# Two transformer blocks on one core: the first norm's root moved behind its projections, and the start reordered

## The reference

```python
def rmsnorm(x, g):
    xf = x.astype(jnp.float32)
    y = xf * lax.rsqrt(jnp.mean(xf * xf, axis=-1, keepdims=True) + EPS)
    return (y * g.astype(jnp.float32)).astype(x.dtype)

u = rmsnorm(h, norm_mix_g[layer])
p = jnp.einsum('bsd,de->bse', u, w_in[layer]) + b_in[layer]
aq, ak, av, hq, hf, hi, hg, gate_a, gate_b = split_columns(p)
y_attn = sliding_window_sink_attention(aq, ak, av, attn_sinks[layer])
y_hgrn = hgrn2_branch(hq, hf, hi, hg, lb_all[layer], hgrn_norm_g[layer])
```

## Time and profile before

| | us |
|---|---|
| median of 3 runs | 791.05 (790.83 to 791.09) |
| the profiled execution | 790.83 |
| its span | 789.1 |
| PE busy | 777.0 (98%) |
| DVE busy | 607.1 (77%) |
| ACT busy | 476.1 (60%) |

### The profile page before, as it was taken

The page is one execution under the profiler, slowest core; times in us unless marked ns, Lnnn a source line. Parts: engine busy times, 40 slices in busy tenths (PEclk is TensorE's granted clock), DMA queues, the critical chain, the costliest instruction groups (busy, mean ns, idle before and its releaser), DMA issues. The chain is left out here.

```text
span 789.1 us, 12516 instructions
## 1 busy us (share of the span) xinstructions
PE 777.0 (98%) x5048; PEld 687.0 (87%) x5048; DVE 607.1 (77%) x815; ACT 476.1 (60%) x727; POOL 18.6 (2%) x38
## 2 busy tenths in 40 slices
PE   8999999999999999999999999999999999999996
PEld 8978978898888898888888888999789999999885
DVE  5587788687887667887869897997878788777464
ACT  6855887568644384444334267876858667665451
POOL 3000002000200000000000000001000000000000
PEclk9999999999999999999999999999999999999999
DMA  8873644656546638799879993644363756555611
GB/s 302 296 261 127 227 138 149 208 186 215 174 161 213 214 107 283 269 305 315 276 242 339 336 380 126 222 135 133 108 213 111 237 175 200 167 172 170 240 53 54
DMA packets 106537, 162.54 MB, mean 206 GB/s; under 512 B 4576, under 2 KB 51824, under 8 KB 106480
## 3 DMA queue, kind: packets, MB, share of 16 engines
q1 hardware_dynamic: 106336, 161.48, 61.3%
q10 hardware_dynamic: 144, 0.26, 0.1%
HBM read 160.67 MB, written 1.06 MB: 205 GB/s over the span
## 5 line engine op out<-in xcount | busy, mean ns | idle before, releaser
L1175 DVE TENSOR_TENSOR wL<-raw,wH 128x2048 fp32r<-128x2048 f32 (+2 forms) x142 | 285.2, 2013 | 84.3 <-ACT wH L764 81.9
L764 ACT ACTIVATE wH<-raw 128x2048 fp32r<-128x2048 f32 (+1 forms) x114 | 212.1, 1864 | 91.7 <-PE ps L1866 61.1
L1863 PE MATMUL ps<-p1H,wH 128*128 128x256 f32 x784 | 224.0, 286 | 1.6 <-DVE arena L1175 0.8
L1863 PE MATMUL ps<-p1H,wL 128*128 128x256 f32 x784 | 221.2, 283 | 0.0
L1863 PE MATMUL ps<-p1L,wH 128*128 128x256 f32 x784 | 219.8, 283 | 0.0
L1863 PEld LDWEIGHTS ps<-p1H,wH 128*128 128x128 f32 x784 | 150.2, 192 | 5.5 <-DVE wL L1175 2.2
L1863 PEld LDWEIGHTS ps<-p1H,wL 128*128 128x128 f32 x784 | 150.2, 192 | 0.0
L1863 PEld LDWEIGHTS ps<-p1L,wH 128*128 128x128 f32 x784 | 149.5, 192 | 0.0
L1866 PE MATMUL ps<-wH,p1H 128*128 128x512 f32 x316 | 125.2, 396 | 0.0
L1866 PE MATMUL ps<-wL,p1H 128*128 128x512 f32 x316 | 123.2, 390 | 0.0
L1866 PE MATMUL ps<-wH,p1L 128*128 128x512 f32 x316 | 123.1, 390 | 0.0
(11 more groups left out here) (303 smaller groups left out, 946.3 us busy)
## 6 DMA issues: line engine op xcount, KB each, us to landing
raw<-in_w_in SPq DMA_DIRECT2D x37, 1024.0 KB, 6.1
raw<-in_w_ada SPq DMA_DIRECT2D x24, 1024.0 KB, 5.2
raw<-in_w_up SPq DMA_DIRECT2D x44, 512.0 KB, 4.7
raw<-in_w_ffn_gate SPq DMA_DIRECT2D x22, 512.0 KB, 4.3
raw<-in_w_ffn_up SPq DMA_DIRECT2D x22, 512.0 KB, 5.5
raw<-in_w_ffn_down SPq DMA_DIRECT2D x10, 1024.0 KB, 5.5
raw<-in_w_down SPq DMA_DIRECT2D x10, 1024.0 KB, 5.1
raw<-in_w_out SPq DMA_DIRECT2D x8, 1024.0 KB, 5.1
```

The lines of the kernel that those rows point to most:

```text
L764: nc.scalar.activation(wH[:, q % NHL, 0:nk, 0:wd], raw[:, i % NRAW, 0:nk, 0:wd], ACT.Copy).then_inc(on.w_hi, 1)
L1175: return v.tensor_tensor(o, a, b, op)
L1863: last = mm(ps[:, t[1], 0:T], wt[:, slot, k, t[2]:t[2] + P], at_[:, k0 + k, :], start=st, stop=en)
```

## The change

1. x is loaded in four channel quarters instead of two token halves, each followed by one block of the first weight panel. The gain's columns of `params` come by a small DMA of their own, the rest of `params` after the first panel.
2. In the first norm (`enter`) ACT writes `p1H = gain * xT` straight from PSUM, and DVE writes `p1L` from PSUM too. No root is needed for that. Squares and roots (`root_0`) come in the event `root`, between the two panels of q0.
3. The root is applied at evacuation. For q, kv, hq and hf DVE multiplies PSUM by the spread root `rbs0` (`rooted`), and ACT then adds the bias from SBUF, or takes the sigmoids. For ga, gb, hi and hg DVE takes root and bias row in one scalar_tensor_tensor.
4. kv comes between q0 and q1; q0 is evacuated one event later, and tiles 0 and 1 of q1, hq and hf (`EARLY`) are evacuated ahead of the split at their last panel. v is transposed into bank 0 and then waits for tile 2 of q1.
5. One sigmoid table serves `c` and the lower bounds, the exponential of `a_log` comes after unit 0. `dtW` is filled in the first FFN and its DMA is issued there. In `hi1` the first `hprep` step comes one panel later.

```diff
-    for _name, _c, _b in (("hi", 3328, 2 - 2 * _i), ("hg", 4352, 2 * _i), ("ga", 5376, 2 * _i), ("gb", 6400, 2 - 2 * _i)):
+        GROUPS[f"{_name}{_i}"] = group("w_in", [(_c + _i * W, W)], cm_tiles(_b, _f), "DDDD", "P1")
+    for _name, _c, _b in (("hi", 3328, 2 - 2 * _i), ("hg", 4352, 2 * _i), ("ga", 5376, 2 - 2 * _i), ("gb", 6400, 2 - 2 * _i)):
...
-GROUPS["kv"] = group("w_in", [(1024, 256)], [("cm", 0, 0), ("cm", 1, P)], "AA", "P1")
+GROUPS["kv"] = group("w_in", [(1024, 256)], [("cm", 4, 0), ("cm", 5, P)], "DD", "P1")
...
+EARLY = ("q1", "hq0", "hf0", "hq1", "hf1")
...
-                tl.append(("evac", name))
-                if name.rstrip("0123456789") in ("f", "u", "xs", "bc", "hf"):
+                (later if name == "q0" else tl).append(("evac", name))
+                if name.rstrip("0123456789") in ("f", "u", "xs", "bc", "hq", "hf"):
...
-    gemm("q0")
-    gemm("q1", [("vectors",)], [("setup",)])
+    gemm("q0", [("root",)])
+    gemm("kv")
     first = X(0, "ga0", 0)
-    gemm("kv", [], first[:-1] + [("v_turn",)] + first[-1:])
+    gemm("q1", [("vectors",), ("setup",)], first[:-1] + [("v_turn",)] + first[-1:] + [("decay",)])
...
-    gemm("hi1", [("hdm", 1), ("hprep", 1, 0)], [("hprep", 1, 1)])
+    gemm("hi1", [("hdm", 1)], [("hprep", 1, 0), ("hprep", 1, 1)])
...
-            for j in range(TB):
-                sp.dma_start(res[:, j], IN["x"][0, j * P:(j + 1) * P, :]).then_inc(on.in_x[j], 16)
-            sp.wait_ge(on.in_x[0], 16)
+            x = IN["x"][0].rearrange("(j p) n -> p j n", p=P)
             for k in range(KP):
+                sp.dma_start(res[:, :, wide(k)], x[:, :, wide(k)]).then_inc(on.in_x[k], 16)
                 sp.dma_start(raw[:, 0, k, :], first[:, k, 0:W]).then_inc(on.in_w0[k], 16)
...
+            def enter():                                   # ScalarE
+                table(ACT.Sqrt)
+                act.wait_ge(on.in_g, 16)
+                for k in range(KD):
+                    if k % 2 == 0:
+                        act.wait_ge(on.ut_psum, k // 2 + 1)
+                    nc.scalar.activation(p1H[:, k], xT(k), ACT.Copy, scale=gain(0, k)).then_inc(on.uh_done, 1)
+                    if k < 4:
+                        first_hi(0, k, 1)
+                    elif k in (4, 5):
+                        first_hi(1, 2 * k - 8, 2)
...
                 if g == "q" and name in ("q0", "q1"):
-                    each(lambda m: aQ[:, 4 * i + m], ACT.Identity, bias=lambda m: pc("b_in", 4 * i + m))
+                    if i == 0:
+                        act.wait_ge(on.in_par, 16)
+                        act.wait_ge(on.rb_psum, 1)
+                        nc.scalar.activation(rbs0, rb, ACT.Copy).then_inc(on.rb_copy, 1)
+                    for m in range(4):
+                        act.wait_ge(*EV[name, m])
+                        nc.scalar.activation(aQ[:, 4 * i + m], aQ[:, 4 * i + m], ACT.Identity,
+                                             bias=pc("b_in", 4 * i + m)).then_inc(on.evac_act, 1)
...
+            def enter():                                   # VectorE
+                dve.wait_ge(on.in_g, 16)
+                for k in range(KD):
+                    if k < 4:
+                        first_lo(0, k, 1, k == 3)
+                    elif k in (4, 6):
+                        first_lo(1, k - 4, 2, k == 6)
+                    dve.wait_ge(on.uh_done, k + 1)
+                    stt(p1L[:, k], xT(k), gain(0, k), p1H[:, k].bitcast(F32), ALU.mult, ALU.subtract).then_inc(on.u_ready, 1)
...
+            def rooted(name, tiles):
+                for m in tiles:
+                    dve.wait_ge(on.tile_done, TILE[name, m])
+                    tt(to[m], ps[:, GROUPS[name]["tiles"][m][1], 0:T], rbs0, ALU.mult).then_inc(on.evac_dve, 1)
...
-                        tt(to, ps[:, GROUPS[name]["tiles"][j][1], :], rows(name)[0], ALU.add).then_inc(on.evac_dve, 1)
+                        stt(to, ps[:, GROUPS[name]["tiles"][j][1], :], R1[:, j:j + 1], rows(name)[0], ALU.mult,
+                            ALU.add).then_inc(on.evac_dve, 1)
...
+                    if e[1] in EARLY and e[2] == 1:
+                        rooted(e[1], range(2))
...
                 elif k == "v_turn":
-                    pe.wait_ge(*EV["kv", 1])
+                    pe.wait_ge(*BIASED["kv", 1])
+                    pe.wait_ge(*EV["q1", 2])
                     for j in range(TB):
-                        last = tr(ps[:, 3, j * P:(j + 1) * P], vT[:, j * P:(j + 1) * P])
+                        last = tr(ps[:, 0, j * P:(j + 1) * P], vT[:, j * P:(j + 1) * P])
```

More of the change, by code:

```diff
@@ L102 @@
           "ga1": (1, 5376 + W), "hi1": (1, 3328 + W), "hg1": (1, 4352 + W)}
+ROOTED = ["kv"] + [f"{_n}{_i}" for _i in range(2) for _n in ("q", "hq", "hf")]
+EARLY = ("q1", "hq0", "hf0", "hq1", "hf1")
 ROWS = 32
@@ L790, in square_x @@
             def square_x(j):
-                act.wait_ge(on.in_x[j], 16)
+                for c in range(4):
+                    act.wait_ge(on.in_x[c], 16)
                 if j:
@@ L1029, in _ @@
                     nc.scalar.activation(lb[:], lbd[:], ACT.Sigmoid).then_inc(on.lb_sig, 1)
-                    nc.scalar.activation(nega[:], pc("a_log", 0, 8), ACT.Exp).then_inc(on.a_exp, 1)
                 if k == "panel":
@@ L1036, in _ @@
                         later_hi(2, 0, 2)
+                elif k == "decay":
+                    nc.scalar.activation(nega[:], pc("a_log", 0, 8), ACT.Exp).then_inc(on.a_exp, 1)
                 elif k == "split":
@@ L1789, in late_turn, with turn_input, spread_roots @@
             def late_turn(n, k):
-                pe.wait_ge(*((on.rb_copy, n + 1) if k == 6 else (on.tmp_done, 8 * n + 2)))
+                pe.wait_ge(*((on.rb_copy, n + 1) if k == 6 else (on.tmp_done, 8 * (n - 1) + 2)))
                 turn(n, (k,), range(TB)).then_inc(on.ut_psum, 1)
+            def turn_input(c):
+                pe.wait_ge(on.in_x[c], 16)
+                if c > 1:
+                    pe.wait_ge(on.u_ready, 2 * c - 2)
+                for k in (2 * c, 2 * c + 1):
+                    for j in range(TB):
+                        last = tr(xT(k)[:, j * P:(j + 1) * P], res[:, j, k * P:(k + 1) * P])
+                last.then_inc(on.ut_psum, 1)
+            def spread_roots(n):
+                for j in range(TB):
+                    pe.wait_ge(on.rd_done, 2 * n + j + 1)
+                    last = spread(rb[:, j * P:(j + 1) * P], R1[:, j:j + 1])
+                last.then_inc(on.rb_psum, 1)
             def gate_sum(g, i):
@@ L1894, in panel @@
                         early = k == 0 and name in NORM_OF
-                        if early:
+                        if q == 0 and k == 0:
+                            pe.wait_ge(on.uh_done, 1)
+                            pe.wait_ge(on.first_hi, 1)
+                            for t in g["tiles"]:
+                                product(t, 0, only=(0,))
+                        elif early:
                             pe.wait_ge(on.uh_done, 8 * NORM_OF[name] + 1)
@@ L1907, in panel @@
                                 pe.wait_ge(on.gate_done, 2 if name == "f0" else 4)
-                            last = product(t, k, only=(0, 2) if early else (0, 1, 2))
+                            last = product(t, k, only=(2,) if early and q == 0 else (0, 2) if early else (0, 1, 2))
                         if early:
```

215 lines of the change are left out of this document (112 added, 103 removed).

## The result

The changed kernel takes 794.24 us (793.94 to 794.97, 4 runs), the kernel before, measured beside it, 790.94 (790.45 to 791.09, 4 runs). The ratio is 1.0042, with a 95% interval of 1.003 to 1.0053, so 2.4 to 4.2 us slower. The forecast was 793.2 within 789.3 to 795.3, slower the likeliest. The sum came out nearly right, but two of its three terms did not: up to unit 0 it had 0.65 and 3.11 were measured, in the second half it had 1.7 and 0.3 were measured.

What follows compares the result with a forecast made beforehand. PE was taken to bound the kernel (busy 777.0 of 789.1 us). Terms 0.65 up to unit 0, 0.1 for later units and 1.7 in the second half sum to 2.45: 790.83 becomes 793.3, median 793.2, range 789.3 to 795.3.

Steps and rivals of the forecast that it cites:

- up to unit 0: From the start to ga0's second panel: start gains 2.4, about 0.5 left after the chain, unit 0 loses 1.15; net +0.65.
- the second half: Second half of the recurrence: added DVE work and waits make k_end 2.7 later; less 1.0 in hand, PE loses 1.7.
- the half megabyte lands at 11.3: Weights in q0: the next half megabyte at 11.3 instead of 13.29, so q0 ends at 19.85, 2.4 gained.
- rival C: Start: quarters of x come at the slow pace, q0 ends at 22.9, total 796.4; chance 0.08.
- The chain: ACT and DVE alternate from q0's end to v_turn: 21.8 long, PE there at 19.1, so PE waits 2.7.
- rival B: At v_turn: chain shorter than PE's way (under 19.1), no 2.7 wait, total 787.8; chance 0.18.
- Part 3: Unit 0: loss of 1.15, net +0.65; exponential table load priced at 1.28 by the row, without a drain.
- Unit 0: Exponentials start 24.95 after q0's end; ga0's second panel at 49.5 against 48.83, +0.65.
- added work 3.65: DVE, second half of the recurrence: eight `rooted` 3.2 plus 0.45 for hQ's products, against 6.58 idle.
- Rival A: Second half of the recurrence: 6.58 idle absorbs 3.65 and the new waits overlap; 0.75 in all, 791.6; chance 0.22.
- Part 4: Second half of the recurrence: +1.7, bounds 0 to 2.6; 0.5 may show earlier, at ba0's first panel.
- theory 1: For both: the two gates go together, ga0's second panel near 50.15, 1.8 us earlier than in the changed kernel; 792.4.

Runs made afterwards that it cites:

- lb_halves: lb_table with x in two channel halves and the first weight panel in two pieces, 512 KB each, instead of quarters; 790.53 us, ratio 0.9994.
- lb_tokens: lb_table with x in two token halves, weights issued right behind without waiting for x to land; 791.38 us, ratio 1.0008.
- late_bias: The changed kernel with ACT's biases of q0 and of kv (with aKS) each one split later; 790.68 us, ratio 0.9995.
- hprep_back: The changed kernel with the first hprep step of the second heads back at its old place, one panel earlier; 798.90 us, ratio 1.0097.
- lb_params: lb_table with the 187 KB of parameters issued behind the first two weight panels instead of ahead of the second; 789.72 us, ratio 0.9986.
- late_vturn: The changed kernel with v's transposes, and PE's wait with them, moved behind ga0's first panel; 796.17 us, ratio 1.0056.
- both: The changed kernel with late_vturn's edit and the exponential table loaded ahead of q1's biases; 794.13 us, ratio 1.0036.
- lb_table: late_bias with the exponential table loaded ahead of q1's biases as well; 789.80 us, ratio 0.9983.
- bef_hprep: The kernel before with only the first hprep step of the second heads moved one panel later; 790.77 us (one run, before 791.01).

## Why the forecast was right in its sum and wrong in two terms

**The step "the half megabyte lands at 11.3" failed by 1.7 us.** It landed at 12.97, 0.3 before its old time. I had taken the gap of 1.4 to 2 us ahead of the weights as gone; it was, but eight small transfers moved 266 GB/s from 2 to 7 us where before, with the gap in it, 285 were moved. The steps behind it held: k=4 started 2.9 us after the landing (forecast 2.75) and q0 ended 8.7 after it, in the changed kernel and in the seven other kernels with quarters alike (landings from 12.24 to 12.97, ends from 20.94 to 21.67). So the forecast's 19.85 was 21.67, past the middle between it and rival C's 22.9. The bounds of that term were right; the value was too near the lower one. The Trainium skill (DMA: Bandwidth & Descriptors, section Bandwidth) spoke for the slower end, and lb_halves agrees in kind (321 against 243 GB/s), but its advice to use large pieces loses here, because the first product waits for them. With lb_halves and lb_tokens the profiles fit a rule with two arms: q0 ends at the later of 8.7 after the half panel and 14.0 after the first product (7.51 + 14.0 = 21.5, 8.40 + 14.0 = 22.4). The second arm is read from these two kernels alone.

**The chain was right.** From q0's end to the wait's end I had 21.8 and it was 43.82 - 21.67 = 22.15; PE itself came at 19.4 instead of 19.1, so the wait was 2.74 for 2.7. late_bias shows the chain to be a matter of order alone. Moving six biases reaches rival B's condition, small work on ACT while DVE writes low parts, and its wait goes, as I wrote for it. Its 787.8 is not reached (789.80 with the early table), since q0 ended at 21.23 there and not at 19.85. No drain was seen behind the table load either: it ends at 45.91 and the next operation starts at 45.93, so Part 3 was right to go by its row.

**Unit 0 was 0.6 us too low.** I had ga0's second panel 29.65 after q0's end and it was 30.27. The exponentials were 25.3 after (24.95 forecast), as the chain came 0.35 later, and the rest is the low clock behind `v_turn`: PE came to `pt` at 51.15, while the second half of the probabilities was ready at 51.09 and the first at 49.77. With the wait PE came late to its own gate. I had priced a wait as its length alone.

**The second half failed: 0.3 for 1.7.** DVE was idle 40.92 - 35.00 = 5.92 in the same stretch, the new waits 2.45 and 3.25 where I said 2.4 and 2.9 to 3.0. The step that failed is "added work 3.65". By the windows DVE is busy only 0.66 more than in the earlier trace rows, 3.0 less than I had. What I took for 34.34 of work held a product of 3.42, and its kind takes 1.22 elsewhere: it stood beside GpSimd's, and by the rows it waited for it. Now that product takes 1.22, which gives 2.2 back. The other 0.8 is work that I priced too high: 0.66 + 2.20 = 2.86 came in, for 3.65. Rival A's figure for this half, nothing, was near, but not its reason: DVE's idle time fell only from 6.58 to 5.92.

```profile
172.08:213.00 40.92, 40.92 (x238) 36.08 (x238) 35.00 (x43) 26.69 (x31) 6.64 (x1) 1.00 0.65 207
```

```profile
193.58 2.29 DVE L1202 TENSOR_TENSOR wL<-raw,wH 128x2048 fp32r<-128x2048 f32 x1 [3.25 <-ACT wH L772]
...
208.44 1.22 DVE L1202 TENSOR_TENSOR arena<-arena 128x1024 f32<-128x1024 f32 x1
```

The last product ends at 213.00, 3.08 after before, the same as PE's own delay, so k_end lost nothing against PE. The 0.3 was lost at ba0's first panel, the place that Part 4 had named for 0.5 of its 1.7: PE's weight load waits there for DVE's low part.

```profile
208.57 0.19 PEld L1941 LDWEIGHTS ps<-wH,pyH 128*128 128x128 f32 x1 [0.39 <-DVE wL L1202]
```

hprep_back shows that without the step's move the root's work would have cost far more there; I had put that move into the sum only by way of the idle time.

**Not forecast:** 0.4 at the first norm of the second block, where PE waits 0.48 for a root. The kernels made from it show 0.1 to 0.9 there, the most in lb_params, and hprep_back 1.8. It varies between kernels whose work there is the same; which transfer or step it is stays open.

In the profiled execution errors of 1.8, 0.6 and 0.4 one way and 1.4 the other left the sum 1.4 short of the 3.8; against the medians it is 1.0 short. It was right in sign for the reason given, ping-pong between ACT and DVE, and in size largely by luck: the second half, which was to bring 1.7 of the 2.45, brought 0.3, and the low clock and the late landing, which were not in the sum, took its place.

## What to carry to other kernels

When a step that one engine did alone is split over two, look at what stands between the hand-overs on each: here the same instructions cost 3.3 us more in one order than in another. Of two gates one behind the other, opening either alone gains nothing, and even both opened gained 0.1 us here, because the wait that moved was followed by a low clock. Read a duration against the shortest of its kind before counting it as work: a product of 3.42 that elsewhere takes 1.22 is likely to hold a wait.

## What the runs showed of the hardware

The clock's price. A wait of 2.74 us was followed by some 3.4 us at half the full clock, eight products 0.2 further apart than their pace, 1.6 us. In late_vturn, with two waits close together, the low stretch came too, and 1.8 us were lost between ga0's second panel (+2.44) and unit 1 (+4.27); in `both`, with waits of 1.47 and 0.67, 1.4. In lb_table, with no wait there, nothing is lost between the two (-1.71 and -1.71). But not every long wait brings it: behind hprep_back's wait of 2.63 at 205.48 the granted clock was 1.00 from 205 to 240. What tells the two apart no run here shows. Executions of one kernel differ too: those of `both` took 792.79, 793.75, 794.13, 794.40 and 795.31 at mean clocks of 0.999, 0.998, 0.997, 0.997 and 0.996, and late_vturn's one at 0.998 took 794.03, where its four at 0.995 and 0.996 took 795.26 to 796.37. So the 792.4 that theory 1 gave `both` was nearly reached where the clock stayed up.

VectorE and GpSimd. GpSimd's product of 128x1024 took 4.42 in the kernel before, bef_hprep and hprep_back, each time with one product of VectorE at 3.42 or 3.43 beside it, and 8.89 in the nine others, where VectorE's took 1.22. The sums fit turns, not sharing: 205.51 - 203.26 = 2.25 for GpSimd while VectorE stands 2.2 still, and in the changed kernel GpSimd ends at 215.25, 2.25 after VectorE's last product at 213.00, and from GpSimd's start up to there VectorE had not paused. No run takes GpSimd's product away, so this is read from the rows and not tested. The Trainium skill (SBUF — State Buffer, section SBUF: two separate sides) says the same: the pair of ports that the two share is locked for a whole instruction. Which of them gets it when both are waiting, no run here settles: in both cases GpSimd started 0.12 us after a split of VectorE. Nor does all of VectorE's work take turns with it: the two instructions at 213.41 in the changed kernel, which read PSUM, took 1.41 with GpSimd's product under way, the same as at 202.65 without it.

```profile
206.36 8.89 POOL L736 TENSOR_TENSOR arena<-arena 128x1024 f32<-128x1024 f32 x1 [67.98 <-DVE arena L1202]
```
